# Gathers of the experts' rows with empty places left out, on one core

## The chip, the cores and the metric

One core of a Trainium2 chip runs the whole program in one launch. The metric is the time of one execution in microseconds (us) on the device. The kernel before was run three times; the median counts.

## The reference

Two transformer blocks in sequence on 512 tokens of width 1024, in float32. The first has a gated linear attention beside a state-space mixer and a product-key layer of 16,384 small experts. The second has a short convolution beside an attention with a forget gate, and then a mixture of 32 experts. Only the last part matters here, cut to its core:

```python
pg = softmax(hf @ w_router_group)             # 4 groups, the best one is taken
le_sel = (hf @ w_router_expert)[group]        # 8 experts in it
e_val, e_idx = lax.top_k(softmax(le_sel), 2)  # 2 experts per token
# every expert, on the tokens that chose it:
y = (silu(x @ w_gate[e]) * (x @ w_up[e])) @ w_down[e]      # 1024 -> 512 -> 1024
out[token] += weight * y
```

512 tokens with two experts each make 1024 rows. Run on its own inputs, the reference gives an expert between 22 and 43 of them; expert 5 has 27, expert 18 has 22, expert 19 has 43.

## The kernel before

All large weights lie in one array, `w_all`, in chunks of 128 x 2048 float32 (1 MB) in the order of use. Each chunk goes through the same steps: SP loads it into a ring; ACT copies it to bfloat16 (`w_hi`, L1693 in the expert stage); DVE subtracts that from the chunk (`w_lo`, L2376); PE multiplies with both parts, three products where float32 had one. `w_hi` and `w_lo` are rings of four. An expert has six chunks: two each for gate, up and down.

**The expert stage** comes last, and works in passes. In one pass every expert gets `CAP` = 64 places, and a further pass runs only if an expert has more than 64 tokens (none here). All 32 experts go through in order, PE, ACT, DVE and POOL each with its own loop over the experts; inside it the order of the work is written out by hand (`step`), and semaphores tie the loops together.

- *SP* (`one_pass`, L539 to L560) loads the stage's 192 chunks into a ring of 12: four places of `w_st`, four in `arena`, `a_hi`, `a_lo`, two in `xn`. One turn of its loop is 12 chunks, two experts. Before each second load it also waits that an earlier pair of loads has landed, so only a few are under way. The two places in `xn` are first loaded once the first two gathers have landed (L552), and everything after them stands behind that in SP's queue.
- *POOL* splits the normalised tokens into two bfloat16 parts and stores them to `x_dram`, 4 KB per token (L667 to L671). Once DVE has the row numbers, it gathers each expert's rows from there by an indirect DMA (`gather`, L674 and L675) into one of two buffers of `x_g`, 64 partitions of 4 KB, one per place. Per expert it copies the next expert's row numbers (`next_rows`, L679), gathers, drains, waits for an expert's outputs and stores 64 x 4 KB to `y_dram` (L689).
- *PE* turns the gathered rows (`expert_rows`, L1244), then does gate, up (L738 to L740) and down (L1281, L1286).
- *ACT* takes the turned rows out (L1697), applies silu (L1702), splits the hidden values (L1706) and moves outputs (L1715).
- *DVE* does the `w_lo` of each chunk, the product with up (L2464), the low part of the hidden values (L2468) and adds an expert's outputs (L2459).

**The row numbers.** The router on DVE (L2379 to L2420) finds each token's two experts, a triangular product on PE its rank within the expert. `rows_of_pass` (L2361) forms `tok_now`, the token's number `tok_f` where the token belongs to this pass, otherwise 0. PE's 16 small products at L1303 sum, for each place and expert, the token numbers that fall on it: a place that no token falls on gets 0. DVE casts the sums to `row_i` (L2474), 64 places x 32 experts. So each empty place has row number 0, and its gather fetches the row of token 0. At the end the outputs of the 1024 real rows are gathered from `y_dram` by place (L726) and added to the residual (L2510). The outputs of empty places are computed and stored too, and nobody reads them.

```python
def gather(p, rows=idx):
    pool.indirect_dma_start(x_g[0:CAP, p, :, :].rearrange("p a d -> p (a d)"), None, x_dram,
                            bass.IndirectOffsetOnAxis(ap=rows[0:CAP, p:p + 1], axis=0)).then_inc(xe_ld[p], 16)
```

Of the kernel before, what the change touches and what calls it, by code (L numbers as in the profile page):

```python
# [11 lines left out]
ALU = mybir.AluOpType  # L12
# [4 lines left out]
T = 512  # L17
TB = T // P
# [24 lines left out]
NE = EG * EPG  # L43
CAP = 64
# [50 lines left out]
DT0 = 32  # L95
EARLY = 6
TD = T - P
T_SPREAD = 2 * P
GT = 48
GATE_TILES = [(0, t) for t in range(0, 40, 8)] + [(1, t) for t in range(80, P, 8)] + [(0, t) for t in range(40, 80, 8)]  # L100
# [53 lines left out]
def build_program(nc, w_all, x_in, cols_in, small_in, rows_in, out):  # L154
    ctx = ExitStack()
    with ctx:  # L156
# [33 lines left out]
        ps = ctx.enter_context(nc.psum_tensor("ps", [P, 8, 512], F32))  # L190
# [4 lines left out]
        def view(at, *shape, dt=F32):  # L195
            n = int(np.prod(shape)) * (2 if dt == BF16 else 4) // 4
            assert at + n <= ARENA, (at, n)
            v = arena[:, at:at + n]
            if dt != F32:
                v = v.bitcast(dt)  # L200
            names = "abcd"[:len(shape)]
            return v.rearrange(f"p ({' '.join(names)}) -> p {' '.join(names)}",
                               **{c: s for c, s in zip(names, shape)}) if len(shape) > 1 else v


        o = 0
# [22 lines left out]
        o = 10 * 1024  # L229
# [14 lines left out]
        o = 16 * 1024 + 4 * P  # L244
# [3 lines left out]
        weight = view(o, SLOTS); o += SLOTS  # L248
        assert o <= 16 * 1024 + 4 * TD
        act_0 = view(16 * 1024 + 4 * TD, SLOTS)  # L250
        gh = view(16 * 1024 + 4 * TD + SLOTS, 2, ROWS)
        v_rows = [view(12 * 1024 + n * D, D) for n in range(4)] + [xn[:, n, :] for n in range(4)]
# [8 lines left out]
        o = 0  # L261
# [26 lines left out]
        tok_f = sb("tok_f", [P, TB])  # L288
# [31 lines left out]
        x_g = view(4096, 2, 2, D, dt=BF16)  # L320
        xeT = view(6144, 2, 2, KT, CAP, dt=BF16)
        o = 0
# [7 lines left out]
        o = TB * 2 * D  # L330
# [22 lines left out]
        blk_f = view(o, 2, 2, TB); o += 4 * TB  # L353
# [3 lines left out]
        now = view(o, 1); o += 1  # L357
        tok_now = view(o, 2, TB); o += 2 * TB
        tok_e = view(o, 2, TB, NE); o += 2 * TB * NE
        n_rows = view(o, 1); o += 1  # L360
        n_rows_i = view(o, 1, dt=I32); o += 1
        row_i = view(o, NE + 1, dt=I32); o += NE + 1
        idx = view(o, 2, dt=I32); o += 2

        ARENA_SLOTS = 4
# [62 lines left out]
        rt_tok, rt_sum, rt_row = sem("rt_tok"), sem("rt_sum"), sem("rt_row")  # L428
        xe_ld = [sem(f"xe_ld{p}") for p in range(2)]
# [142 lines left out]
        def _(pool):  # L572
# [92 lines left out]
            for tb in range(TB):  # L665
                pool.wait_ge(xn_done, 5 * TB + tb + 1)
                pool.tensor_copy(pk[:, tb, 0, :], xn[:, tb, :]).then_inc(pk_hi, 1)  # L667
                pool.wait_ge(pk_hi, tb + 1)
                pool.tensor_tensor(pk[:, tb, 1, :], xn[:, tb, :], pk[:, tb, 0, :], ALU.subtract).then_inc(pk_lo, 1)
                pool.wait_ge(pk_lo, tb + 1)  # L670
                pool.dma_start(x_dram[tb * P:(tb + 1) * P, :], pk[:, tb, :, :].rearrange("p a d -> p (a d)")).then_inc(x_st, 16)  # L671
            pool.wait_ge(x_st, 16 * TB)

            def gather(p, rows=idx):  # L674
                pool.indirect_dma_start(x_g[0:CAP, p, :, :].rearrange("p a d -> p (a d)"), None, x_dram,  # L675
                                        bass.IndirectOffsetOnAxis(ap=rows[0:CAP, p:p + 1], axis=0)).then_inc(xe_ld[p], 16)

            def next_rows(i, c):
                pool.tensor_tensor(idx[0:CAP, c % 2:c % 2 + 1], row_i[0:CAP, bass.ds(2 * i + c, 1)], zero_i[0:CAP, 0:1], ALU.add)  # L679
# [1085 lines left out]
        def _(dve):  # L1765
# [45 lines left out]
            for half in range(2):  # L1811
                rows = slice(half * GC, (half + 1) * GC)
# [4 lines left out]
            d = slice(DT0, DT0 + SH)  # L1817
# [61 lines left out]
            for tb in range(TB):  # L1879
                b = (tb % 2) * 3  # L1880
# [66 lines left out]
            for g in range(2):  # L1947
                ahead(C_WOUT + 2 * g)
                for tb in range(TB):
                    dve.wait_ge(tok_done, TB * (G_WOUT + g) + tb + 1)  # L1950
                    s = slice(g * 512, (g + 1) * 512)
# [174 lines left out]
            for n in range(N_U):  # L2126
# [4 lines left out]
                if unit is not None:  # L2131
                    best_keys(unit % PH)
                    if unit % PH == PH - 1:
                        b = unit // PH
# [3 lines left out]
                if n in SOFT_END_AT:  # L2138
                    b = SOFT_END_AT[n]
# [208 lines left out]
            for g in range(2):  # L2348
                ahead(C_WO2 + 2 * g)
                for tb in range(TB):  # L2350
                    dve.wait_ge(tok_done, TB * (G_WO2 + g) + tb + 1)
                    s = slice(g * 512, (g + 1) * 512)
# [8 lines left out]
            def rows_of_pass(r):  # L2361

                if not isinstance(r, int):
                    dve.tensor_scalar(now, now, 1.0, None, ALU.add)
                    dve.drain()
                for s in range(2):
                    dve.scalar_tensor_tensor(tok_now[:, s, :], blk_f[:, 0, s, :], now, tok_f[:, :], ALU.is_equal, ALU.mult)
                dve.drain()
                dve.tensor_tensor(tok_e.rearrange("p s t e -> p (s t) e"), e_one.rearrange("p s t e -> p (s t) e"),
                                  tok_now.rearrange("p s t -> p (s t)").unsqueeze(2).to_broadcast([P, 2 * TB, NE]), ALU.mult).then_inc(rt_tok, 1)  # L2370
# [6 lines left out]


            dve.memset(lr_g, LOWEST)  # L2379
            dve.wait_ge(rt_mm, 1)  # L2380
            dve.tensor_copy(lr, ps[:, 2, 0:TB * SM_R].rearrange("p (t n) -> p t n", t=TB))
            dve.drain()
# [87 lines left out]
            def first(r):  # L2470
                if not isinstance(r, int):
                    rows_of_pass(r)
                dve.wait_ge(rt_sum, r + 1)
                dve.tensor_copy(row_i[0:CAP, 0:NE], ps[0:CAP, 5, 0:NE]).then_inc(rt_row, 1)  # L2474
                if not isinstance(r, int):
                    lo_of(r, 0, 0)
                lo_of(r, 0, 1)
                for k in range(2, 5):
                    lo_of(r, 0, k)
                lo_of(r, 0, 5)  # L2480
                hidden(r, 0, 0, 2)
                lo_of(r, 0, 6)
# [131 lines left out]
```

## Time and profile before

| | |
|---|---|
| median of 3 runs | 2750.77 us (2747.97 to 2754.58) |
| profiled execution | 2743.79 us; its span, first to last instruction, 2742.1 us |
| PE busy | 2588.0 us, 94% |
| DVE busy | 1962.7 us, 72% |
| ACT busy | 1252.2 us, 46% |
| POOL busy | 1008.0 us, 37% |
| HBM read / written | 539.59 MB / 73.53 MB |

The profile describes one execution. Busy shares are over the whole span, while the expert stage takes about a fifth of it, from some 2165 us on; it is read by stretches. A DMA share is the mean over the core's 16 DMA engines of the time that their packets took, and goes slightly over 1 where packets overlap. Queue q1 holds SP's loads, q0 what POOL issues. In a timeline, "[idle before <-releaser]" is the time that the engine stood idle before the instruction and what ended it. A load, gather or store is issued by an instruction that is short; the transfer goes on after it.

### The profile page before, as it was taken

What the parts mean: (1) busy time and instruction counts of PE and PEld (TensorE: products, weight loads), DVE (VectorE), ACT (ScalarE), POOL (GpSimd) and SP (SyncE); (2) the same over time, 40 slices, a digit from 0 to 9 for tenths busy, and PEclk for the clock granted to TensorE, in tenths of its full rate; (3) what the DMA queues carried; (4) which work ended last, traced back from release to release, by engine and by line L of the source; (5) the groups of instructions that cost most, each with busy time, mean ns of one, the idle gap of its engine ahead of it and who ended that gap; (6) DMA issues with size and microseconds to landing.
All of it is one profiled execution on the core that took longest, in us unless ns stands there. A gap on an engine that the chain in (4) does not pass through costs nothing. (4 is left out here: it accounts for less than half of the span.)

```text
span 2742.1 us, 38302 instructions
## 1 busy us (share of the span) xinstructions
PE 2588.0 (94%) x13813; PEld 1281.3 (47%) x13813; DVE 1962.7 (72%) x3255; ACT 1252.2 (46%) x1316; POOL 1008.0 (37%) x724
## 2 busy tenths in 40 slices
PE   8989999999999999999999899999999699998994
PEld 4465444444444544444444454555544344444441
DVE  5545887988855635888888754466543699999996
ACT  5434323323234432333333343444432589888884
POOL 0000000177776746888888200000001355334331
PEclk9989999999999999999999999999999799999997
DMA  5301874344446478999999532221113599999995
GB/s 215 108 16 55 287 280 182 120 161 147 170 146 153 163 182 284 364 366 362 366 365 365 216 125 94 91 75 65 62 67 141 224 393 393 392 393 402 398 389 191
DMA packets 175580, 614.83 MB, mean 224 GB/s; under 512 B 58336, under 2 KB 74720, under 8 KB 125792
## 3 DMA queue, kind: packets, MB, share of 16 engines
q1 hardware_dynamic: 57312, 411.62, 39.6%
q0 software_dynamic: 47712, 127.12, 12.8%
q10 hardware_dynamic: 70432, 74.46, 8.9%
q8 instruction: 76, 1.25, 0.2%
q14 instruction: 48, 0.39, 0.0%
HBM read 539.59 MB, written 73.53 MB: 224 GB/s over the span
## 5 line engine op out<-in xcount | busy, mean ns | idle before, releaser
L738 PE MATMUL ps<-a_hi,w_hi 128*128 128x512 bf16 (+3 forms) x1768 | 648.3, 369 | 8.0 <-ACT xn L1499 2.9
L740 PE MATMUL ps<-a_hi,w_lo 128*128 128x512 bf16 (+3 forms) x1768 | 648.6, 369 | 0.0
L739 PE MATMUL ps<-a_lo,w_hi 128*128 128x512 bf16 (+3 forms) x1768 | 648.6, 369 | 0.0
L738 PE MATMUL ps<-w_hi,arena 128*128 128x512 bf16 (+1 forms) x1344 | 514.0, 382 | 11.9 <-DVE arena L2176 9.9
L739 PE MATMUL ps<-w_lo,arena 128*128 128x512 bf16 (+1 forms) x1344 | 512.3, 381 | 0.0
L740 PE MATMUL ps<-w_hi,arena 128*128 128x512 bf16 (+1 forms) x1344 | 512.2, 381 | 0.0
L2026 DVE TENSOR_TENSOR w_lo<-w_st,w_hi 128x2048 bf16<-128x2048 f32 x127 | 290.5, 2290 | 221.8 <-ACT w_hi L1493 122.6
L1493 ACT ACTIVATE w_hi<-w_st 128x2048 bf16<-128x2048 f32 x127 | 242.4, 1909 | 337.9 <-PE ps L740 305.1
L624 POOL DMA_INDIRECT gate_dram<-arena x256 | 321.2, 1255 | 85.4 <-issue 79.3
L1499 ACT ACTIVATE xn<-ps 128x512 f32<-128x512 f32 x128 | 76.2, 597 | 440.9 <-PE ps L740 334.7
L738 PEld LDWEIGHTS ps<-a_hi,w_hi 128*128 128x128 bf16 x1768 | 173.4, 98 | 194.1 <-issue 9.7
L740 PEld LDWEIGHTS ps<-a_hi,w_lo 128*128 128x128 bf16 x1768 | 173.3, 98 | 193.8 <-issue 0.3
L639 POOL DMA_INDIRECT arena<-act_dram,h_idx x128 | 248.9, 1944 | 39.0 <-issue 39.0
L739 PEld LDWEIGHTS ps<-a_lo,w_hi 128*128 128x128 bf16 x1768 | 173.2, 98 | 181.2 <-issue 0.3
L1774 DVE TENSOR_TENSOR w_lo<-w_st,w_hi 128x2048 bf16<-128x2048 f32 x68 | 155.0, 2287 | 121.7 <-ACT w_hi L1337 121.6
L738 PEld LDWEIGHTS ps<-w_hi,arena 128*128 128x128 bf16 (+1 forms) x1344 | 138.1, 103 | 177.0 <-issue 16.3
L740 PEld LDWEIGHTS ps<-w_hi,arena 128*128 128x128 bf16 (+1 forms) x1344 | 138.4, 103 | 154.1 <-issue 3.1
L739 PEld LDWEIGHTS ps<-w_lo,arena 128*128 128x128 bf16 (+1 forms) x1344 | 138.3, 103 | 146.0 <-issue 2.9
L667 POOL CAST arena<-xn 128x1024 bf16<-128x1024 f32 x4 | 4.1, 1037 | 546.3 <-DVE xn L1788 546.3
L1337 ACT ACTIVATE w_hi<-w_st 128x2048 bf16<-128x2048 f32 x68 | 129.1, 1905 | 98.6 <-PE ps L740 96.9
L616 POOL DMA_DIRECT2D act_dram<-xn x64 | 36.0, 562 | 336.4 <-ACT xn L1499 318.6
L2376 DVE TENSOR_TENSOR w_lo<-arena,w_hi 128x2048 bf16<-128x2048 f32 x64 | 146.0, 2281 | 17.3 <-ACT w_hi L1693 17.3
(410 smaller groups left out, 4069.9 us busy)
## 6 DMA issues: line engine op xcount, KB each, us to landing
w_st<-in_w_all SPq DMA_DIRECT2D x260, 1024.0 KB
arena<-in_w_all SPq DMA_DIRECT2D x64, 1024.0 KB
act_dram<-xn POOLq DMA_DIRECT2D x64, 512.0 KB
xn<-in_w_all SPq DMA_DIRECT2D x32, 1024.0 KB
arena<-act_dram ACTq DMA_DIRECT2D x64, 384.0 KB
gate_dram<-xn ACTq DMA_DIRECT2D x14, 1536.0 KB, 8.4
arena<-gate_dram ACTq DMA_DIRECT2D x64, 336.0 KB
a_hi<-in_w_all SPq DMA_DIRECT2D x16, 1024.0 KB
```

The source lines that it names most:

```text
L616: pool.dma_start(act_dram[n], u_st[:, n % 2, :, :].rearrange("p j t -> p (j t)")).then_inc(u_stored[n % 2], 16)
L624: pool.indirect_dma_start(gate_cells, bass.IndirectOffsetOnAxis(ap=place[:, b, j:j + 1], axis=0), shared[:, b, j:j + 1], None).then_inc(g_ ...
L639: pool.indirect_dma_start(act_0[:, k:k + 1], None, acts, bass.IndirectOffsetOnAxis(ap=h_idx[:, k:k + 1], axis=0)).then_inc(act_ld[k // ROW ...
L738: pe.matmul(dst, l_hi, r_hi, start=start, stop=False)
L739: pe.matmul(dst, l_hi, r_lo, start=False, stop=False)
L740: return pe.matmul(dst, l_lo, r_hi, start=False, stop=stop)
L1337: act.activation(dst, w_st[:, n % RING, :], ACT.Copy).then_inc(w_hi_done, 1)
L1493: act.activation(w_hi[:, s, :], w_st[:, s, :], ACT.Copy).then_inc(w_hi_done, 1)
L1499: act.activation(u_st[:, n % 2, t, :], ps[:, t, :], ACT.Gelu).then_inc(u_out, 1)
L1774: dve.tensor_tensor(lo_n, w_st[:, n % RING, :], hi_n, ALU.subtract).then_inc(w_lo_done, 1)
L2026: dve.tensor_tensor(w_lo[:, s, :], w_st[:, s, :], w_hi[:, s, :], ALU.subtract).then_inc(w_lo_done, 1)
L2376: dve.tensor_tensor(w_lo[:, s, :], moe_st[k % MOE_RING], w_hi[:, s, :], ALU.subtract).then_inc(w_lo_done, 1)
```

## The change

The token numbers are summed with one added, so that a place without a token is told from token 0 by its sum 0. DVE then subtracts the one and adds 4096 where the sum was 0. The gather gets a bound, 511: an index above it is not an error and is skipped. The places of `x_g` that are skipped keep what they held, so POOL first clears both buffers. `tok_1` and `row_n` are new small tensors. The same 64 places of every expert are computed and stored as before.

```diff
--- before.py
+++ after.py
@@ -95,6 +95,7 @@
 DT0 = 32
 EARLY = 6
 TD = T - P
+NO_ROW = 4096
 T_SPREAD = 2 * P
 GT = 48
 GATE_TILES = [(0, t) for t in range(0, 40, 8)] + [(1, t) for t in range(80, P, 8)] + [(0, t) for t in range(40, 80, 8)]
@@ -360,6 +361,8 @@
         n_rows = view(o, 1); o += 1
         n_rows_i = view(o, 1, dt=I32); o += 1
         row_i = view(o, NE + 1, dt=I32); o += NE + 1
+        row_n = view(o, NE); o += NE
+        tok_1 = view(o, TB); o += TB
         idx = view(o, 2, dt=I32); o += 2
 
         ARENA_SLOTS = 4
@@ -669,11 +672,14 @@
                 pool.tensor_tensor(pk[:, tb, 1, :], xn[:, tb, :], pk[:, tb, 0, :], ALU.subtract).then_inc(pk_lo, 1)
                 pool.wait_ge(pk_lo, tb + 1)
                 pool.dma_start(x_dram[tb * P:(tb + 1) * P, :], pk[:, tb, :, :].rearrange("p a d -> p (a d)")).then_inc(x_st, 16)
+            pool.memset(x_g[0:CAP, :, :, :].rearrange("p b a d -> p (b a d)"), 0.0)
+            pool.drain()
             pool.wait_ge(x_st, 16 * TB)
 
             def gather(p, rows=idx):
                 pool.indirect_dma_start(x_g[0:CAP, p, :, :].rearrange("p a d -> p (a d)"), None, x_dram,
-                                        bass.IndirectOffsetOnAxis(ap=rows[0:CAP, p:p + 1], axis=0)).then_inc(xe_ld[p], 16)
+                                        bass.IndirectOffsetOnAxis(ap=rows[0:CAP, p:p + 1], axis=0),
+                                        bounds_check=T - 1, oob_is_err=False).then_inc(xe_ld[p], 16)
 
             def next_rows(i, c):
                 pool.tensor_tensor(idx[0:CAP, c % 2:c % 2 + 1], row_i[0:CAP, bass.ds(2 * i + c, 1)], zero_i[0:CAP, 0:1], ALU.add)
@@ -2364,7 +2370,7 @@
                     dve.tensor_scalar(now, now, 1.0, None, ALU.add)
                     dve.drain()
                 for s in range(2):
-                    dve.scalar_tensor_tensor(tok_now[:, s, :], blk_f[:, 0, s, :], now, tok_f[:, :], ALU.is_equal, ALU.mult)
+                    dve.scalar_tensor_tensor(tok_now[:, s, :], blk_f[:, 0, s, :], now, tok_1[:, :], ALU.is_equal, ALU.mult)
                 dve.drain()
                 dve.tensor_tensor(tok_e.rearrange("p s t e -> p (s t) e"), e_one.rearrange("p s t e -> p (s t) e"),
                                   tok_now.rearrange("p s t -> p (s t)").unsqueeze(2).to_broadcast([P, 2 * TB, NE]), ALU.mult).then_inc(rt_tok, 1)
@@ -2377,6 +2383,7 @@
 
 
             dve.memset(lr_g, LOWEST)
+            dve.tensor_scalar(tok_1, tok_f[:, :], 1.0, None, ALU.add)
             dve.wait_ge(rt_mm, 1)
             dve.tensor_copy(lr, ps[:, 2, 0:TB * SM_R].rearrange("p (t n) -> p t n", t=TB))
             dve.drain()
@@ -2471,7 +2478,9 @@
                 if not isinstance(r, int):
                     rows_of_pass(r)
                 dve.wait_ge(rt_sum, r + 1)
-                dve.tensor_copy(row_i[0:CAP, 0:NE], ps[0:CAP, 5, 0:NE]).then_inc(rt_row, 1)
+                dve.tensor_scalar(row_n[0:CAP, :], ps[0:CAP, 5, 0:NE], 0.0, float(NO_ROW), ALU.is_equal, ALU.mult)
+                dve.drain()
+                dve.scalar_tensor_tensor(row_i[0:CAP, 0:NE], ps[0:CAP, 5, 0:NE], -1.0, row_n[0:CAP, :], ALU.add, ALU.add).then_inc(rt_row, 1)
                 if not isinstance(r, int):
                     lo_of(r, 0, 0)
                 lo_of(r, 0, 1)
```

## Rows read from the trace of the kernel before

**Rows 1.** The page, section 2: busy tenths in 40 slices, DMA engines

```profile
DMA  5301874344446478999999532221113599999995
```

**Rows 2.** Busy time by stretch; columns named in its head: engines, clock, DMA share, GB/s

```profile
2250.00:2300.00 50.00, 47.91 (x273) 22.66 (x272) 48.75 (x29) 44.95 (x36) 25.86 (x10) 1.00 1.02 397
...
2600.00:2650.00 50.00, 44.67 (x244) 20.66 (x243) 44.51 (x26) 41.62 (x33) 18.00 (x9) 0.97 1.02 392
```

**Rows 3.** Waits in 2150:2742: waiting <- waited for: us in total, times, longest us

```profile
DVE w_lo L2376 <- ACT w_hi L1693: 45.6, 52, 7.7
...
ACT w_hi L1693 <- DMA w_st<-in_w_all: 11.3, 13, 2.6
```

**Rows 4.** Timeline of SP's queue, first load of a turn: start us, us, instruction

```profile
2201.14 0.94 SPq L560 DMA_DIRECT2D w_st<-in_w_all  x2
...
2651.51 0.33 SPq L560 DMA_DIRECT2D w_st<-in_w_all  x1
```

**Rows 5.** Timeline of DVE, outputs added: experts 1, 11, 30 and 31

```profile
2207.02 1.21 DVE L2459 TENSOR_TENSOR arena<-ps,arena 64x1024 f32<-64x1024 f32 x1
...
2368.18 1.21 DVE L2459 TENSOR_TENSOR arena<-ps,arena 64x1024 f32<-64x1024 f32 x1
...
2695.05 1.21 DVE L2459 TENSOR_TENSOR arena<-ps,arena 64x1024 f32<-64x1024 f32 x1
...
2708.77 1.22 DVE L2459 TENSOR_TENSOR arena<-ps,arena 64x1024 f32<-64x1024 f32 x1 [7.64 <-ACT arena L1715]
```

**Rows 6.** DMA, 2226.5:2233 (a store), then 2220:2226.5 (gather of expert 5)

```profile
DMA packets 415, 2.74 MB, mean 421 GB/s; under 512 B 49, under 2 KB 49, under 8 KB 113
...
q1 hardware_dynamic: 335, 2.47, 91.1%
q0 software_dynamic: 80, 0.26, 10.0%
...
DMA packets 359, 2.29 MB, mean 352 GB/s; under 512 B 48, under 2 KB 48, under 8 KB 112
...
q1 hardware_dynamic: 279, 2.02, 87.8%
q0 software_dynamic: 80, 0.26, 13.8%
```

**Rows 7.** DMA, 2434.5:2441 (gather of expert 18), then 2449.5:2456 (expert 19)

```profile
DMA packets 355, 2.26 MB, mean 348 GB/s; under 512 B 47, under 2 KB 47, under 8 KB 111
...
DMA packets 372, 2.39 MB, mean 368 GB/s; under 512 B 48, under 2 KB 48, under 8 KB 112
```

**Rows 8.** The gather's line L675; POOL's and PE's timeline around the gather of expert 6

```profile
L675 POOL DMA_INDIRECT arena<-x_dram,arena x32: 902/5590/5611, 2153.7 to 2651.6; - x32
...
DMA to landing us min/median/max: 4.1/12.5/13.1
...
2226.89 0.58 POOL L689 DMA_DIRECT2D y_dram<-arena  x1 [7.87 <-issue]
...
2229.54 5.60 POOL L675 DMA_INDIRECT arena<-x_dram,arena  x1 [0.15 <-issue]
...
2247.22 0.46 PE L1244 MATMUL ps<-ident_b,arena 64*128 64x64 bf16 x10
```

**Rows 9.** Timeline ahead of the stage (POOL, DVE), POOL's largest memset, DVE's L1788

```profile
2136.84 0.56 POOL L671 DMA_DIRECT2D x_dram<-arena  x1 [0.30 <-POOL arena L669]
...
2139.47 0.31 DVE L2381 COPY arena<-ps 128x144 f32<-128x144 f32 x1 [0.95 <-PE ps L740]
...
2153.23 0.18 DVE L2474 CAST arena<-ps 64x32 int32<-64x32 f32 x1 [0.55 <-PE ps L1303]
...
L583 POOL MEMSET arena<- 128x512 f32 x1 | 0.6, 555 | 0.0
...
2119.51 1.84 DVE L1788 SCALAR_TENSOR_TENSOR xn<-res,rstd,row 128x1024 f32<-128x1024 f32 x1
...
L1788 DVE SCALAR_TENSOR_TENSOR xn<-res,rstd,row x20: 1283/1285/1843, 8.4 to 2737.8; 128x1024 f32<-128x1024 f32 x20
```

## The prediction, made before the change was run

> **What bounds the kernel now.** I read the page's slices first, then the stage's waits, then the DMA packets, stretch by stretch. In the page's 40 slices the change can only reach the last fifth: its DMA row stands at 9 in the 33rd to the 39th slice [rows 1]. That is the expert stage, some 2165 to 2700 us. Two stretches of 50 us are compared [rows 2]. In 2250:2300 the DMA engines are saturated, and DVE is busy 48.75 us of 50. In 2600:2650 the DMA share is the same, but DVE has fallen to 44.51 us and PE from 47.91 to 44.67 us, at nearly the same rate of 392 to 397 GB/s. So the early experts go at DVE's pace and the late ones at the transfers' pace. The waits agree: ACT's splits of weight chunks wait for the loads, 11.3 us in all at the places in `w_st` alone, and DVE's `w_lo` waits for ACT behind them, 45.6 us [rows 3].
>
> Two periods measure it. SP issues the loads of two experts in one turn of its loop; the turns at 2201.14 and 2651.51 lie 13 turns apart, 34.64 us each, so **17.32 us per expert** is what the transfers take [rows 4]. DVE adds one output per expert at L2459: from expert 1 (2207.02) to expert 11 (2368.18) ten steps take 161.16 us, **16.12 us each** [rows 5]. The last expert is added at 2708.77. At DVE's pace throughout it would be 2368.18 + 19 x 16.12 + 13.72 (the last step, 2695.05 to 2708.77) = 2688.1. The transfers thus cost **20.7 us** of the end, and no change to the transfers can bring more than that. The loads begin with a lead: it lasted about 12 experts of 1.20 us, so about 14.4 us.
>
> **What a gather costs.** A gather and a store of one expert's outputs both move 64 rows of 4 KB by the same queue, q0: 80 packets, 0.26 MB. In 6.5 us around a store the engines move 421 GB/s and the store takes 10.0% of their time. In 6.5 us around the gather of expert 5 they move 352, and the gather takes 13.8% [rows 6]. The shortfall is (421 - 352) x 6.5 = 0.45 MB, or 1.07 us; with its own 0.26 MB (0.62 us) a gather takes **1.69 us** of all transfers. The period confirms it: 6.29 MB of weights, 0.26 MB of store, at 421 GB/s, and 1.69 us make 17.25, against 17.32 measured.
>
> Is it the repeated reading of one row? Every empty place now fetches token 0's row. By the reference on its own inputs the experts hold 22 to 43 tokens, 1024 in all of 32 x 64 places, so there is one pass and half the rows are empty. Expert 18 (22 tokens, 42 empty places) gives 348 GB/s, expert 5 (37 empty) 352 and expert 19 (21 empty) 368 [rows 6, 7]. Twice the empty places makes a shortfall of 0.47 instead of 0.34 MB. Read as a line, 21 empty places more cost 0.13 MB or 0.31 us, so 32 of them 0.47 us, and the other 0.60 us of the shortfall belongs to the gather as such.
>
> **The change, part by part.**
>
> *Rows skipped.* Half of the rows drop out. If the whole cost goes with the number of rows, a gather becomes 1.69 / 2 = 0.85 us cheaper. Bounds: if only the bytes count, 0.31; if the shortfall hung on the empty rows, 0.31 + 1.07 = 1.38. By the line through experts 18 and 19 it would be 0.31 + 0.47 + 0.30 = 1.08. I take 0.85, the lower of the two that rest on rows 6 and 7. The period of the transfers falls to 16.47 us. That is still 0.35 over DVE's pace, but over 30 experts it eats 10.5 us of a lead of 14.4, so the loads stop deciding. The full 20.7 us come off. The break-even is a saving of 1.20 - 14.4/30 = 0.72 us per gather. What is late next is DVE, at 48.75 of 50 us busy.
>
> *Gather on POOL.* The gather's instruction takes 5.6 us at most (median 5.59, shortest 0.90) and its rows land 12.5 us after issue (median); the gather issued at 2229.54 is used by PE at 2247.22 [rows 8]. No row shows a gather with a bound. The nearest is this one: I bound the comparison by 0 and by the whole shortest instruction, 0.9 us. Both cost the end nothing: 2247.22 - 2229.54 - 12.5 leaves 5.2 us of slack, and POOL idles 7.87 us before its store [rows 8]. 0; what lies beyond is the slower rival.
>
> *First rows.* DVE's cast of the row numbers (0.18 us, L2474) becomes two operations with a drain between; POOL's first gather waits for it, PE for the gather, and SP for the first two gathers before it loads into `xn` and starts the long stream of loads [rows 9]. One more operation like it, 0.18, and the drain between them, estimated at under half of that: +0.25 us, all on the path. The first gather's own transfer halves, 0.62 us to 0.31: -0.3 (bounds 0 and -0.6).
>
> *Memset of `x_g`.* POOL clears 4096 bf16 per partition after its last store is issued (2137.40). A memset of 512 float32 took 0.56 us, so 1.1 ns an element: 4.4 us, or 2.2 if two elements go at once. It ends at 2139.6 to 2141.8; POOL itself then only waits for the row numbers, cast at 2153.23, which covers it. The danger is DVE: at 2139.47 it starts the router's chain, which is on the path [rows 9]. DVE has been held by POOL in this trace: its product L1788 takes 1.285 us (median), but 1.84 us at 2119.51, beside a product of POOL's (L669) [rows 9]. I take +0.2, between 0 and 2.3 us.
> The Trainium skill (SBUF — State Buffer, Who interferes with whom) states that a GpSimd operation and a DVE copy or tensor_scalar in a two-port mode exclude each other for the whole instruction, while an operation of DVE with two SBUF inputs is held only by a GpSimd operation that reads. By that rule the new `tok_1` would wait out the memset, 2.3 us instead of 0.2, and the sum would be -18.4; the row shows a POOL operation that reads holding one of DVE with two inputs, and no run here shows a memset doing it.
>
> *`tok_1`.* One tensor_scalar of 128x4 while DVE waits 0.95 us for PE: hidden, 0; without that cover 0.2.
>
> **Sum:** -20.7 + 0.25 - 0.3 + 0.2 = -20.5 us. The profiled execution took 2743.8 us (span 2742.1), which gives 2723.3. It lies 7.0 below the median of the three runs, 2750.8, so I carry the difference over: 2730.3, said as 2730.5. Some 0.2% (5.5 us) is what can be told from no change here.
>
> **Rivals.**
> 1. *Part of the saving* (0.21). The skipped rows save less than 0.72 us. With bytes alone (0.31) the transfers run at 17.01; 30 x 0.89 - 14.4 = 12.3 us stay late, gain 8.4: 2742. With 0.5, gain 14: 2737. For it: the shortfall's cause isn't seen in any row. Against: expert 18 and 19.
> 2. *Nothing* (0.13). Either an empty row still is a packet, or the load that counts stays. The gather is 64 rows and 16 writes of 4 B, so 16 engines with four rows each [rows 6]. If an engine has four neighbouring rows, those with rows 0 to 19 are full for every expert (22 is the fewest), and a weight load ends with its slowest engine. If the slowdown stays on those as well, 0 gained: 2751. For it: no view tells the engines apart. Against: on those engines the rows are 4 x 4 KB of some 400 KB per expert, while the slowdown hits weights too (q1's share falls from 91.1 to 87.8% but its bytes from 2.47 to 2.02 MB); with half the engines free of gather it should shrink, and it need only lose 0.72 of 1.07.
> The Trainium skill (DMA: Bandwidth & Descriptors, Why a DMA increments its semaphore by 16 and not by 1) says that a transfer goes to the largest number of engines up to 16 that divides its partitions, which is this split; the 80 packets agree. It doesn't say which rows are together.
> 3. *Slower* (0.06). The comparison makes POOL's gather long. POOL is busy 25.86 us of 50 [rows 2], 8.3 us per expert; it becomes the bound, over today's 17.32, when the gather grows by 9.0 us, 0.14 us per row. Each us beyond costs 31: at +10 us, 2751 + 31 = 2782. For it: no row shows a bounded gather. Against: it needs ten times the shortest instruction of today, 0.90 us [rows 8].
>
> **Chances and range.** Forecast, gain 17 to 22 us: 0.60; rivals 0.21, 0.13, 0.06. The forecast's own values are 2729 to 2734, and a median of runs wanders by 2 or 3 us, which gives 2727 below; the part saving reaches 2744 to 2745. What lies above has 0.19. Both gaining cases exceed 5.5 us: faster 0.81; same 0.13; slower 0.06.
>
> **What would show it.** Around a gather q0 should show some 27 + 16 packets for expert 5 instead of 80, and the rate should be near 385 GB/s instead of 352, the steps at L2459 16.12 us to the end, ACT's waits for loads almost gone, SP waiting for `w_lo` instead. The cast's successor starts at most 1 us later than 2153.23. I am wrong if q0's packets are unchanged (rival 2), if the loads' turns stay at 34 us or more with fewer packets (rivals 1 and 2), or if PE waits for gathers past the first (rival 3).

## The result: faster by 0.9%, past the low end of the range

| | before | after |
|---|---|---|
| median | 2751.73 us (4 runs, 2747.97 to 2754.58) | 2725.74 us (4 runs, 2722.78 to 2731.51) |
| profiled execution | 2743.79 us | 2726.76 us |
| span | 2742.1 us | 2725.1 us |
| expert stage, first to last output added | 517.87 us | 497.07 us |

The ratio is 0.9909, with an interval of 0.9888 to 0.9930. The prediction was 2730.5 us, 2727 to 2745: 1.3 us too high at its low end. The direction came out, and so did what bounds the stage before and after; the number did not.

The page of the kernel after, busy tenths of the DMA engines in 40 slices, against [rows 1]: the stage is as full as before, and shorter.

```profile
DMA  5301774344445567999999732212114399999995
```

The stretches of [rows 2] after the change (PE, PEld, DVE, ACT, POOL, granted clock, DMA share, GB/s):

```profile
2250.00:2300.00 50.00, 46.98 (x282) 22.84 (x286) 48.76 (x29) 44.94 (x34) 26.63 (x10) 1.00 1.01 402
...
2600.00:2650.00 50.00, 47.24 (x270) 22.86 (x272) 48.75 (x29) 43.75 (x34) 27.58 (x10) 1.00 1.01 406
```

The early stretch had 397 GB/s and has 402, the late one had 392 and has 406. DVE is busy 48.75 us of 50 in the late stretch too, where it had fallen to 44.51.

The waits of 2150:2725 that answer to [rows 3] (total us, times, longest):

```profile
DVE w_lo L2382 <- ACT w_hi L1699: 25.6, 34, 7.1
...
ACT w_hi L1699 <- DMA w_st<-in_w_all: 1.9, 2, 1.4
```

DVE's wait for ACT is 20.0 us shorter, and ACT's wait for loads in `w_st` fell from 11.3 to 1.9 us. The stage lost about as much, which DVE's own outputs show best. The timeline of DVE after, outputs of experts 0, 1, 11 and 31 added, against [rows 5], and under it the first output before:

```profile
2195.05 1.21 DVE L2466 TENSOR_TENSOR arena<-ps,arena 64x1024 f32<-64x1024 f32 x1
...
2211.16 1.21 DVE L2466 TENSOR_TENSOR arena<-ps,arena 64x1024 f32<-64x1024 f32 x1
...
2372.30 1.21 DVE L2466 TENSOR_TENSOR arena<-ps,arena 64x1024 f32<-64x1024 f32 x1
...
2692.12 1.22 DVE L2466 TENSOR_TENSOR arena<-ps,arena 64x1024 f32<-64x1024 f32 x1 [7.49 <-ACT arena L1721]
```

```profile
2190.90 1.21 DVE L2459 TENSOR_TENSOR arena<-ps,arena 64x1024 f32<-64x1024 f32 x1
```

The steps are 16.11 or 16.12 us up to expert 28, as the first eleven were before; then come 16.73, 15.61 and 13.56. Only one step is late. The last output less the first is 497.07 us instead of 517.87: **20.8 us less**, where the prediction had 20.7.

The transfers' own pace, from the first load of a turn of SP's loop and the same load 13 turns on, against [rows 4]:

```profile
2203.57 0.34 SPq L563 DMA_DIRECT2D w_st<-in_w_all  x1
...
2636.46 0.33 SPq L563 DMA_DIRECT2D w_st<-in_w_all  x1
```

That is 432.89 us for 26 experts, 16.65 each, against 17.32: a gather became 0.67 us cheaper, where 0.85 was forecast and 0.72 was called the break-even. By the prediction's own rule the loads lose 16.65 - 16.12 = 0.53 us per expert against DVE, 14.3 us in 27 experts, so a lead of 14.4 lasts to expert 27, and the late step of 16.73 is where it ends. In this execution the cap was reached with nothing to spare.

A window of 6.5 us around the landing gather of expert 5, against [rows 6], and the gather's line against [rows 8]:

```profile
DMA packets 415, 2.54 MB, mean 391 GB/s; under 512 B 91, under 2 KB 91, under 8 KB 118
...
q1 hardware_dynamic: 335, 2.43, 95.9%
q0 software_dynamic: 80, 0.11, 5.9%
```

```profile
L680 POOL DMA_INDIRECT arena<-x_dram,arena x32: 931/5630/5647, 2159.4 to 2636.5; - x32
...
DMA to landing us min/median/max: 3.0/11.9/12.8
```

The rate went from 352 to 391 GB/s, but q0 still has 80 packets: a skipped row still is a packet, of a few bytes instead of 4 KB (91 packets are under 512 B instead of 48), and the bytes fell from 0.26 to 0.11 MB, which is the 27 rows. The gather's instruction takes 5.63 us against 5.59 in the median.

Last, what was added ahead of the stage, against [rows 9]. The timeline of POOL and DVE after:

```profile
2141.17 3.54 POOL L675 MEMSET arena<- 64x4096 bf16 x1
...
2142.34 0.09 DVE L2385 MEMSET arena<- 128x32 f32 x1
2142.34 2.39 DVE L2386 TENSOR_SCALAR arena<-tok_f 128x4 f32<-128x4 f32 x1
2143.38 1.36 DVE L2388 COPY arena<-ps 128x144 f32<-128x144 f32 x1
...
2158.16 0.18 DVE L2481 TENSOR_SCALAR arena<-ps 64x32 f32<-64x32 f32 x1 [0.55 <-PE ps L1309]
2158.42 0.18 DVE L2483 SCALAR_TENSOR_TENSOR arena<-ps,arena 64x32 int32<-64x32 f32 x1
2158.53 4.47 DVE L2382 TENSOR_TENSOR w_lo<-w_st,w_hi 128x2048 bf16<-128x2048 f32 x2
```

```profile
2138.44 0.09 DVE L2379 MEMSET arena<- 128x32 f32 x1
```

The second fence is the kernel before. `tok_1`, 128x4 elements, took 2.39 us: it ends at 2144.73, with the memset (2144.71). The copy of the router's numbers behind it ends at 2144.74; before it took 0.31 us. From the memset of `lr_g` to the end of that copy it was 2139.47 + 0.31 - 2138.44 = 1.34 us and is 2.40: the memset cost **1.06 us** up to here, and with the second operation the row numbers are written 16.26 us after the memset of `lr_g` instead of 14.97, +1.29.

The spans then add up. DVE's memset of `lr_g` stands ahead of everything changed and came 3.90 us later in this execution. From there to the first output it was 52.46 us and is 52.71: +0.25. The stage is -20.80, what follows the last output -0.35. The sum is -17.0, the difference of the spans. Without the 3.90 that arose ahead of the change, -20.55 is left up to the last output; the medians say -26.0.

### The profile page after: what moved, and what is told of

It is laid out like the page before. It is cut to its first block and busy times, and to the rows that moved or that the text cites. A ratio compares the mean times of both kernels' runs of the same rounds, so it can differ in the third digit from the quotient of the medians.

```text
span 2725.1 us, 38116 instructions
## 1 busy us (share of the span) xinstructions
PE 2565.1 (94%) x13590; PEld 1280.7 (47%) x13813; DVE 1963.7 (72%) x3257; ACT 1248.8 (46%) x1316; POOL 1053.7 (39%) x725
## 5 line engine op out<-in xcount | busy, mean ns | idle before, releaser
L745 PE MATMUL ps<-a_lo,w_hi 128*128 128x512 bf16 (+2 forms) x1747 | 640.9, 369 | 3.9 <-issue 0.3
L746 PE MATMUL ps<-a_hi,w_lo 128*128 128x512 bf16 (+2 forms) x1745 | 640.5, 369 | 1.3 <-DVE xn L2327 0.2
L744 PE MATMUL ps<-a_hi,w_hi 128*128 128x512 bf16 (+2 forms) x1698 | 622.5, 369 | 9.1 <-ACT xn L1505 2.9
L744 PE MATMUL ps<-w_hi,arena 128*128 128x512 bf16 (+1 forms) x1326 | 507.0, 382 | 12.3 <-DVE arena L2182 7.8
L745 PE MATMUL ps<-w_lo,arena 128*128 128x512 bf16 (+1 forms) x1327 | 505.9, 381 | 1.0
L746 PE MATMUL ps<-w_hi,arena 128*128 128x512 bf16 (+1 forms) x1327 | 505.5, 381 | 0.9
L680 POOL DMA_INDIRECT arena<-x_dram,arena x32 | 165.0, 5157 | 14.8 <-DVE arena L2483 9.2
```

The costliest lines, as they stand in the source:

```text
L744: pe.matmul(dst, l_hi, r_hi, start=start, stop=False)
L745: pe.matmul(dst, l_hi, r_lo, start=False, stop=False)
L746: return pe.matmul(dst, l_lo, r_hi, start=False, stop=stop)
```

## The experiments

All ratios are to runs of the kernel before on the same chip. The first question was the 5 us between the forecast of -20.5 and the measured -26.0.

**The kernel before, again.** No edit.

> The kernel before, unchanged, to see how its executions scatter and where. Theory A (the change brings 20.5 us, the cap set by DVE's pace, and the other 5 us of the measured 26 are scatter of the runs outside the expert stage): ratio 1.000 within 0.002; its profile has the step of one expert at 17.3 us once the lead is gone and expert 31's output added 517 to 519 us after expert 0's, as in the first profile (517.9), whatever its whole time is. Theory B (most executions of the kernel before have slower transfers than the profiled one, which the change takes away too): the expert stage of this profile is several us longer than 517.9 us.

2747.48 us (12 runs); ratio 1.0003, interval 0.9992 to 1.0014. Another 23 runs of the kernel before on the same chip have a median of 2745.85 and lie between 2740.85 and 2750.82. So single executions scatter over 10 us, and the first three, at 2750.77, were 4.9 us above this median. The profile has late steps from expert 12 on, as the first, and a stage of 519.88 us, 2.0 longer than the first: a little above theory A's 517 to 519, and not the several us of theory B.

**The change, again.** No edit.

> The changed kernel, unchanged, with more rounds. Theory A: ratio 0.9925 (20.5 us less), within 0.001. Theory B: 0.990 to 0.991 (25 us or more less). Both: outputs of experts 16.11 us apart from 1 to 28, 497 us from the first to the last.

2724.55 us; ratio 0.9921, interval 0.9908 to 0.9933, -21.7 us by the ratio and -21.3 by the medians. The forecast of -20.5 us as a ratio is 0.9925. The stage in the two profiles is 519.88 against 499.61 us, -20.3. Here a step of 17.63 us is late (experts 25 to 26), so the cap isn't quite reached in every execution; a stage varies by 2 us or so, and the 20.8 of the first pair is that near to 20.7 partly by luck. The time after is the same as at first (2725.74); the time before was what stood too high.

**Bounds, memset and sums kept, nothing skipped.**

```diff
-NO_ROW = 4096
+NO_ROW = 1
```

> The changed kernel, but an empty place asks for row 0, within the bound, as before: all 64 rows are fetched; memset, extra operations and the bound stay. My theory (the time comes from rows not fetched, the rest costs 1.3 us: 1.03 of the memset holding DVE's tok_1 and 0.26 of the second operation on the row numbers): the kernel before plus about 1.3 us, ratio 1.0005; 64 rows of 4 KB per gather. Rival (the bounded form of the gather is itself gentler on the other transfers): clearly below 1, 0.995 or less.

Empty places fetch token 0 again. Ratio 1.0009, interval 0.9997 to 1.0021; the stage takes 519.44 us. The rate of 2200:2650 is that of before:

```profile
DMA packets 26651, 177.12 MB, mean 394 GB/s; under 512 B 3336, under 2 KB 3336, under 8 KB 6728
```

The whole gain comes from the rows that are not fetched, and the rest of the change costs less than the times of whole runs can tell.

**The memset as float32.**

```diff
-pool.memset(x_g[0:CAP, :, :, :].rearrange("p b a d -> p (b a d)"), 0.0)
+pool.memset(x_g[0:CAP, :, :, :].rearrange("p b a d -> p (b a d)").bitcast(F32), 0.0)
```

> The changed kernel with the memset of the two buffers written as 2048 float32 instead of 4096 bfloat16 per partition. If POOL's memset costs by the element, it takes 1.8 us instead of 3.54 and ends about 0.5 us after DVE's tok_1 would start, so that the router's first copy starts without delay: tok_1 takes some 0.7 us instead of 2.39 and 1.0 us comes off the path. If it costs by the byte, nothing changes. In the whole time 1 us is hardly to be told: ratio 0.9925 or 0.992 by theory A of the first run.

Its timeline of POOL and DVE, the same instructions as above:

```profile
2139.82 1.83 POOL L675 MEMSET arena<- 64x2048 f32 x1
...
2140.82 0.85 DVE L2386 TENSOR_SCALAR arena<-tok_f 128x4 f32<-128x4 f32 x1
2141.86 0.31 DVE L2388 COPY arena<-ps 128x144 f32<-128x144 f32 x1 [0.18 <-PE ps L746]
```

The memset is half as long, `tok_1` again ends with it (2141.67 and 2141.65), and now within DVE's idle time before the copy. From the memset of `lr_g` (2140.82) to the copy's end it is 1.35 us, as before the change. The price up to the copy, and its cause, are shown. In the total it can't be seen (2724.70 us against 2724.55 of the change): ratio 0.9920, interval 0.9907 to 0.9933.

The second question was why a gather costs more than its bytes, and what fewer rows do to that.

**A quarter of the rows skipped.** Only the empty places 48 to 63 carry the index past the last token (no expert has more than 43 tokens); the other empty places fetch token 0.

```diff
+pool.memset(far[:, :], 1.0)
+pool.affine_select(out=far[:, :], in_=far[:, :], compare_op=ALU.is_ge, fill=float(NO_ROW), base=47,
+                   pattern=[[0, 1]], channel_multiplier=-1)
-dve.tensor_scalar(row_n[0:CAP, :], ps[0:CAP, 5, 0:NE], 0.0, float(NO_ROW), ALU.is_equal, ALU.mult)
+dve.tensor_scalar(row_n[0:CAP, :], ps[0:CAP, 5, 0:NE], 0.0, far[0:CAP, 0:1], ALU.is_equal, ALU.mult)
```

> The changed kernel with only the empty places 48 to 63 skipped: 16 x 32 = 512 rows, half of the 1024 empty ones; the others fetch row 0 as before. My theory (cost by the row, rows spread over the 16 DMA engines, a lead of 14.4 us that the transfers' excess over DVE's pace must eat first): the measured saving of the full change, 17.32 - 16.65 = 0.67 us per gather, halves to 0.34; transfers at 16.98 us per expert, 0.87 x 30 - 14.4 = 11.7 us stay late, so 9 us less than the kernel before, plus 1.3 of own cost: ratio about 0.997. Rival (an engine has four neighbouring rows, and the slowest engine decides): places 48 to 63 are four engines' rows, the other twelve keep theirs, so no gain: 1.0005. Rival (no lead, gain simply proportional): 0.9965, not to be told from mine by the time; by the trace: with a lead the late steps begin around expert 16, without one at the first.

Ratio 1.000, interval 0.9989 to 1.0011. Nothing is gained: 16 rows fewer, and the rate fell with the bytes. DMA in 2200:2650:

```profile
DMA packets 26703, 175.41 MB, mean 390 GB/s; under 512 B 3780, under 2 KB 3780, under 8 KB 6804
```

My expectation, a part of the gain, was wrong. It is not the number of rows that counts.

**Another row for each empty place.** Place p fetches token p instead of token 0.

```diff
-dve.tensor_scalar(row_n[0:CAP, :], ps[0:CAP, 5, 0:NE], 0.0, float(NO_ROW), ALU.is_equal, ALU.mult)
+dve.tensor_scalar(row_n[0:CAP, :], ps[0:CAP, 5, 0:NE], 0.0, tok_1[0:CAP, 0:1], ALU.is_equal, ALU.mult)
```

> The changed kernel, but an empty place p asks for token p's row, within the bound: all 64 rows are fetched, and none of them many times. Against the run without skipping, where the empty places all fetch row 0, it tells what the repeated row costs. If the shortfall of a gather comes from the repeated row (0.47 of its 1.07 us by the line through experts 18 and 19): transfers at 16.85, 7 us of stall left, ratio 0.995. If it doesn't: the same as without skipping, 1.0005, steps late from expert 12 on.

Ratio 1.0012, interval 1.0002 to 1.0023. Reading one row many times costs no more than reading 64 different ones; the line through experts 18 and 19 in the prediction [rows 6, 7] was no evidence of it.

**No row fetched at all.** Every index lies past the last token, so the experts' inputs are zeros.

```diff
-dve.scalar_tensor_tensor(row_i[0:CAP, 0:NE], ps[0:CAP, 5, 0:NE], -1.0, row_n[0:CAP, :], ALU.add, ALU.add).then_inc(rt_row, 1)
+dve.scalar_tensor_tensor(row_i[0:CAP, 0:NE], ps[0:CAP, 5, 0:NE], float(NO_ROW), row_n[0:CAP, :], ALU.add, ALU.add).then_inc(rt_row, 1)
```

> The changed kernel with 4096 added to every row number, so that all rows of all gathers are skipped and no token row is fetched at all; the experts work on the cleared buffers. It tells what is left to gain in the gathers' transfers. If DVE's pace is the bound (my theory): every step 16.11 us, 497 us from the first output to the last, 0.99 to 0.992 in all, at most 2.5 us below the changed kernel, whose other two profiles have 1.2 to 3 us of late steps. If the transfers still decide: another 10 us or more off, ratio below 0.988.

2721.52 us; ratio 0.9909, interval 0.9889 to 0.9929. No step to expert 28 is over 16.2 us, ACT's splits no longer wait for any load, and the stage takes 497.92 us. Twice the saving of rows brings no more in the stage than the change (497.07 and 499.61): DVE bounds it. SP's loads now wait 263 us for DVE's `w_lo`, and still the DMA share is 1.01 in 2250:2300, at 401 GB/s. So a share of 1.01 doesn't tell that the transfers are the bound; the steps and the waits do.

**The same bytes into 128 partitions.** Each gather fetches 128 half rows of 2 KB into 128 partitions; the second half of `x_g` stays as it is, and the rows are fixed ones instead of the expert's.

```diff
-pool.indirect_dma_start(x_g[0:CAP, p, :, :].rearrange("p a d -> p (a d)"), None, x_dram,
-                        bass.IndirectOffsetOnAxis(ap=rows[0:CAP, p:p + 1], axis=0),
-                        bounds_check=T - 1, oob_is_err=False).then_inc(xe_ld[p], 16)
+pool.indirect_dma_start(x_g[:, p, 0, :], None, x_dram.rearrange("t (a d) -> (t a) d", a=2),
+                        bass.IndirectOffsetOnAxis(ap=tok_i[:, 0:1], axis=0)).then_inc(xe_ld[p], 16)
```

> Each gather moves the same 0.26 MB as 128 rows of 2 KB into 128 partitions instead of 64 rows of 4 KB into 64; the row numbers are fixed (0 to 127), and the second half of each place's row isn't loaded, so this leaves out the routing of the rows and computes on others. No skipping. If the shortfall comes from 16 engines writing into only 64 partitions: no dip in the rate around a gather, weight packets near 313 ns throughout, transfers at 17.32 - 1.07 = 16.25, ratio near 0.991. If it comes from the reads (rows of the gather in memory) or from the indirect transfer as such: as without skipping, 1.0005 or a little above for twice the packets.

2724.61 us; ratio 0.9913, interval 0.9895 to 0.9931. DMA in 2200:2650:

```profile
GB/s 422 421 420 420 422 422 419 421 420 420 420 422 420 421 422 419 419 424 420 419 418 423 418 422 422 419 422 423 419 419 419 422 418 422 424 418 422 422 420 419
DMA packets 28437, 189.34 MB, mean 421 GB/s; under 512 B 3553, under 2 KB 3553, under 8 KB 7100
...
q0 software_dynamic: 4441, 14.53, 8.1%
```

In no slice is there a dip left, though a gather moves its full 0.26 MB. So the shortfall belongs neither to the bytes nor to the indirect transfer as such. The rows' source differs too (fixed rows that lie one behind the other), but which rows are read made no difference where place p fetched token p. The number of packets doesn't differ: q0's 4441 are 160 for each gather with its store, as before, so the view doesn't show the half rows as packets of their own. What is left is writing into 64 partitions only. That is the whole gain of the change by another way, with nothing skipped.

**Which 32 rows.** Three kernels fetch exactly 32 rows for every expert and differ only in the places. `far` is 0.0 for a place that is fetched and 4096.0 for one that is skipped; tokens on skipped places are left out. `tok_1` is the token's number itself here.

```diff
-dve.tensor_scalar(tok_1, tok_f[:, :], 1.0, None, ALU.add)
+dve.tensor_scalar(tok_1, tok_f[:, :], 0.0, None, ALU.add)
-dve.tensor_scalar(row_n[0:CAP, :], ps[0:CAP, 5, 0:NE], 0.0, float(NO_ROW), ALU.is_equal, ALU.mult)
+dve.tensor_scalar(row_n[0:CAP, :], ps[0:CAP, 5, 0:NE], 0.0, 0.0, ALU.is_equal, ALU.mult)
-dve.scalar_tensor_tensor(row_i[0:CAP, 0:NE], ps[0:CAP, 5, 0:NE], -1.0, row_n[0:CAP, :], ALU.add, ALU.add).then_inc(rt_row, 1)
+dve.scalar_tensor_tensor(row_i[0:CAP, 0:NE], ps[0:CAP, 5, 0:NE], far[0:CAP, 0:1], row_n[0:CAP, :], ALU.add, ALU.add).then_inc(rt_row, 1)
```

> Exactly 32 of the 64 places of every expert are fetched, places 0 to 31; places 32 to 63 carry an index past the last token (tokens beyond 32 are left out, empty places among the 32 fetch token 0). The three kernels of this call with 32 rows differ only in which places. Theory P (the shortfall arises where a place p and the place p+32 of the same gather are written at the same time): no pair is left, so the shortfall falls to 0.2 us or less, the transfers need about 16.1 us per expert, the gain is the whole cap: ratio 0.9915 (0.990 to 0.993), rate around a gather 410 GB/s or more. Theory N (each engine has four neighbouring rows, and the fullest engine counts): engines 0 to 7 keep all four of their rows, nothing is gained: ratio 1.000, as with the quarter skipped. Theory R (the number of rows alone): half of the shortfall, a saving of 0.85 us per gather: ratio 0.9925.

> Also exactly 32 places, 0 to 15 and 32 to 47 (the other tokens are left out). Theory P: all 32 rows are in pairs p and p+32, on half of the ways; the fullest way carries as much as before, so the shortfall stays at 0.8 to 1.0 us, only the bytes are saved (0.31 us), and the ratio is 0.998 to 1.000. Theory N: eight engines full and eight empty, as with places 0 to 31, so the same ratio as that kernel. Theory R: 0.9925, as that kernel.

> Again exactly 32 places, 0 to 15 and 48 to 63: as many in the upper half as in the kernel with pairs, but no place p with its place p+32 (the other tokens are left out). Theory P: as with places 0 to 31, shortfall 0.2 us or less, ratio 0.9915. Theory N: the same as the other two. A third reading, that rows in the upper half as such are the slow ones, gives the same ratio as the kernel with pairs and a worse one than places 0 to 31. So P alone has this one fast and the one with pairs slow.

Measured: places 0 to 31, ratio 0.9920 (0.9905 to 0.9935), stage 496.95 us. Places 0 to 15 and 32 to 47, ratio 0.9990 (0.9980 to 0.9999), stage 519.26. Places 0 to 15 and 48 to 63, ratio 0.9935 (0.9920 to 0.9950), stage 503.08. The DMA engines in 2200:2650, in this order:

```profile
DMA packets 27984, 182.38 MB, mean 405 GB/s; under 512 B 4402, under 2 KB 4402, under 8 KB 7045
...
q0 software_dynamic: 4432, 10.83, 6.7%
```

```profile
DMA packets 26731, 173.87 MB, mean 386 GB/s; under 512 B 4215, under 2 KB 4215, under 8 KB 6802
...
q0 software_dynamic: 4310, 10.60, 6.7%
```

```profile
DMA packets 27551, 179.45 MB, mean 399 GB/s; under 512 B 4319, under 2 KB 4319, under 8 KB 6975
...
q0 software_dynamic: 4400, 10.89, 6.8%
```

The gathers' own packets take the same share in all three, 6.7 to 6.8%. What differs is what the weights' loads beside them get. The same view gives the transfers' period of each kernel, as bytes per expert (six chunks of 1.049 MB, a store of 0.262 MB, the gathered rows) over the mean rate. Less the 15.57 us that chunks and store take at 421 GB/s, it is what one gather costs. Three more profiles of the change's gathers (the change again, `tok_1` in the setup, the float32 memset) give 16.63 to 16.66 us per expert, so the figure repeats within a few hundredths. The kernel that fetches nothing isn't in the table, since its loads wait for DVE; in the last row they wait 42 us for it in all, so 0.63 is an upper bound.

| kernel | rows fetched | MB in 450 us | us per expert | a gather costs |
|---|---|---|---|---|
| before | 64 | 177.33 | 17.30 | 1.73 us |
| nothing skipped | 64 | 177.12 | 17.32 | 1.75 |
| token p in place p | 64 | 176.07 | 17.42 | 1.85 |
| places 48 to 63 skipped | 48 | 175.41 | 17.32 | 1.75 |
| places 0-15, 32-47 | 32 | 173.87 | 17.30 | 1.73 |
| places 0-15, 48-63 | 32 | 179.45 | 16.76 | 1.20 |
| after | 32 in the mean | 180.91 | 16.63 | 1.06 |
| places 0-31 | 32 | 182.38 | 16.49 | 0.93 |
| 128 partitions, half rows | 64 | 189.34 | 16.20 | 0.63 |

The first five fetch 64, 64, 64, 48 and 32 rows and cost the same within 0.12 us. They have in common that both place p and place p + 32 are fetched for p = 0 to 15. Where no such pair is left the cost is 0.93 or 1.20 us. So **what counts first is whether places p and p + 32 are both fetched, even for a quarter of the 64**, not the number of rows, nor how they lie in fours beside each other, nor how many are in the upper half.

The change itself shows it, expert by expert. SP's first loads into `xn` of a turn after the change, in its timeline:

```profile
2230.66 1.61 SPq L563 DMA_DIRECT2D xn<-in_w_all  x2
...
2332.98 0.86 SPq L563 DMA_DIRECT2D xn<-in_w_all  x2
...
2466.90 0.86 SPq L563 DMA_DIRECT2D xn<-in_w_all  x2
...
2631.37 0.86 SPq L563 DMA_DIRECT2D xn<-in_w_all  x2
```

In the three turns between the first two lines the gathers of experts 6 to 11 land, which have 36 to 42 tokens each by the reference; a turn takes 34.11 us. In the five between the last two those of experts 20 to 29 land, with 23 to 31 tokens and so no pair; a turn takes 32.89. That is 0.61 us per gather, while the 11 rows between them are 0.11 us of bytes. With nothing skipped the same two stretches take 34.49 us a turn each.

It isn't known what p and p + 32 share: a way into SBUF or a DMA engine. No view tells the 16 engines apart. The store, 64 rows of 4 KB by the same queue, leaves the rate at 421 GB/s [rows 6], which speaks against the engine. My expectation of 0.2 us or less beyond the bytes was too bold: a row alone on its way still costs about half of two (0.93 against 1.73), and 0.93 - 0.31 = 0.6 us lies beyond its bytes.

The Trainium skill (SBUF — State Buffer, Door 1: The DMA port swizzle) says that DMA reaches SBUF by 16 ports of eight partitions each, that partitions 4k to 4k + 3 share one with those 32 higher, and that partitions 0 to 63 reach only eight of the 16. By that, a gather before puts 32 KB on each of eight ports and none on the others; skipping places 48 to 63, or keeping the pairs, leaves four ports at 32 KB; places 0 to 31 put 16 KB on each of the eight, and 128 half rows 16 KB on each of all 16. The table agrees in the main: the kernels with 32 KB on their fullest port cost most. With the page's 27.2 GB/s per port, 32 KB would be 1.20 us, an estimate, against 1.73 measured. It doesn't say why 0-15 with 48-63 costs 0.27 us more than 0-31, since it has both at 16 KB on eight ports, nor why 0-31 costs 0.30 more than 128 half rows, which put 16 KB on their fullest port too. Both stay open.

**`tok_1` out of the way.** POOL makes `tok_1` once in the setup, and the memset is float32.

```diff
+pool.iota(tok_1i[:, :], [[P, TB]], base=1, channel_multiplier=1)
+pool.tensor_copy(tok_1[:, :], tok_1i[:, :])
-dve.tensor_scalar(tok_1, tok_f[:, :], 1.0, None, ALU.add)
```

> The change, with its two costs ahead of the stage removed: tok_1 is made once by POOL in the setup instead of on DVE behind the router's start, and the clearing of the rows' buffers is written as float32 (half as many elements). Expected: the memset on POOL 1.83 us instead of 3.54, DVE's first copy of the router no longer behind tok_1, 1.0 us less between the memset of lr_g and the first w_lo (15.2 us instead of 16.2). Ratio 0.992 (0.9905 to 0.9935); 1.0 us is 0.04%, which the runs hardly tell from the change itself (0.9921). The theory that the late steps of the stage eat an earlier start (the loads' lead shrinks with it) gives the same ratio as the change.

2725.61 us; ratio 0.9918, interval 0.9904 to 0.9931. DVE in its timeline, where nothing stands between the memset of `lr_g` and the copy:

```profile
2139.49 0.09 DVE L2388 MEMSET arena<- 128x32 f32 x1
2140.53 0.31 DVE L2390 COPY arena<-ps 128x144 f32<-128x144 f32 x1 [0.95 <-PE ps L749]
```

To the copy's end it is 1.35 us instead of 2.40, as expected. From the memset of `lr_g` to the first output it is 52.24 us instead of 52.71 (52.80 in the change's second profile, 50.80 with the float32 memset alone), so this distance itself varies by more than the 1.05 us. In the total it isn't told from the change.

## Why the prediction was right in its working and wrong in its number

- **The bound and the cap: right.** Late experts went at the transfers' pace, and DVE's 16.12 us was next. Predicted -20.7 us, measured -20.8 and -20.3. The kernel that fetches nothing shows that no more was there in the stage. One reading behind it was no evidence: the DMA share of 1.02 [rows 2], since it is 1.01 in that kernel too.
- **The step that failed is the carry-over:** "It lies 7.0 below the median of the three runs, 2750.8, so I carry the difference over", with "a median of runs wanders by 2 or 3 us". The profiled execution of before, 2743.79, was an ordinary one: 23 runs have their median at 2745.85, 15 on another chip at 2748.68, 23 on a third at 2746.70. It was the three runs that were high, by 2 to 5 us, while the runs after were not (2725.74 at first, 2724.55 and 2725.61 in later runs of the change and of its variant); whether the three were high by chance or by the chip isn't shown. The sum of -20.5 against the profiled execution gave 2723.3, and that is within 2.5 us of the 2725.74 measured; against the median of 23 runs it gives 2725.4, while 2730.3 is 4.6 off. So the number failed by the base that the sum was put on, and the other terms below, some of them wrong, add up to little. In the nine profiles whose setup wasn't edited the memset of `lr_g`, ahead of all that was edited, lies between 2137.71 and 2143.09 us: so a part of the scatter arises there. The low end of the range left 3.5 us for it.
- **The saving per gather: mis-sized.** Predicted 0.85 us, half of the cost for half of the rows; measured 0.67. The premise, "the whole cost goes with the number of rows", was wrong: 48 rows cost what 64 do. An expert with up to 32 tokens fills only places 0 to 31, and by the reference 16 of the 32 experts have no more; the other 16 still fetch some pairs. 0.67 was below the break-even of 0.72, and the cap was reached all the same, since a shortage of 0.53 us per expert takes 27 experts to use up the lead.
- **The gather on POOL: right,** 5.63 us in the median against 5.59, and no wait of PE's for a gather but the first.
- **First rows: right, +0.25.** Two operations of 0.18 us at 2158.16 and 2158.42 where one stood: +0.26.
- **The first gather: -0.3 predicted, -0.6 measured,** at the end of its bounds. From the written row numbers to PE's first product on the rows it is 8.21 us before, 8.22 with nothing skipped, 7.56 and 7.67 in the two profiles after, and 6.42 with nothing fetched. Up to that product it comes to +0.64 (23.82 us after the memset of `lr_g` instead of 23.18): +1.29 up to the row numbers and -0.65 behind them. Up to the first output it is +0.25. The rest isn't assigned: that stretch takes 29.28 and 29.23 us before, 28.89 and 28.83 after, and 28.03 with nothing skipped, where the first output comes no later than before (52.35 against 52.46) though both costs are there.
- **The memset: wrong, +0.2 predicted, +1.06 measured,** inside its bounds. The rule that the prediction set beside it was right and the row that I preferred was of another kind: `tok_1` was held until POOL's memset ended. The Trainium skill (SBUF — State Buffer, Who interferes with whom) states this for a tensor_scalar in a two-port mode; the end of `tok_1` within 0.02 us of the memset's agrees, though the trace doesn't show the mode. Its price was 1.06 and not 2.3 us, since the copy behind `tok_1` would have waited 0.95 us for PE anyway.
- **SP waiting for `w_lo`:** hardly. SP's queue waits 7.2 us for it in all (1.9 before); loads are still paced by earlier loads, as they are 0.53 us per expert slower than DVE.
- **Rival 1** (part of the saving) was near: one step more late, and it would have begun. **Rival 2** was half right: an empty row is still a packet, of a few bytes; and "the load that counts stays" is what the quarter skipped showed. It failed because half of the experts have no token on a place above 31, and its ground, that an engine sets the pace when its four neighbouring rows are full, is refuted: 32 rows in fours, in places 0-31, gain all. **Rival 3** had no ground: the comparison costs POOL's instruction nothing that shows.

## What to carry to other kernels

Here a gather into 64 partitions slowed the loads beside it by more than its bytes, and most where p and p + 32 were both written: try 128 partitions with half rows, or the rows in the lowest 32, before counting bytes. Where two engines are within a few per cent of each other, work out the cap and the break-even first; beyond the cap a bigger saving buys nothing. And forecast a change as a difference to many runs, or as a ratio: three runs of a kernel that scatters over 10 us are a weak base for an absolute time.

## What the runs showed of the hardware that I had not expected

- A row that a bounded gather skips leaves a packet of a few bytes: 80 packets with 27 rows fetched as with 64. With all rows skipped q0's 7.35 MB in 2200:2650 are the 28 stores of 0.262 MB, 7.34, and next to nothing else.
- 32 rows in places 0-15 and 32-47 cost the transfers 1.73 us, as 64 rows do; 32 rows in places 0-31 cost 0.93; 128 half rows, as many bytes as before, 0.63, which is about their bytes alone (0.62). Stores of 64 x 4 KB leave the rate at 421 GB/s [rows 6].
- The DMA share stays at 1.01 when SP's loads wait 263 us for DVE (nothing fetched).
- DVE's operation on 128x4 elements took 2.39 us beside a memset on POOL, and 0.85 us beside one that is 1.7 us shorter.
- A memset on POOL of the same bytes takes 3.54 us as 64x4096 bf16 and 1.83 us as 64x2048 float32: 0.86 and 0.89 ns per element of a partition.
